# Weight remainders written over the raw unit: five raw slots and four high slots, loads released by TensorE

## What is computed

```
def first_block(x, ...):
    for layer in range(2):
        hn = rms_norm(h, norm_g[layer])
        if layer % 2 == 0:  y = pool_mixer(hn, ...)    # (m * silu(gate)) @ w_out, m from a windowed mean and w_grp
        else:               y = hgrn2_mixer(hn, ...)   # gated linear recurrence over chunks, 16 heads of 128
        h = h + y
    return rms_norm(h, final_g)

def second_block(x, c, ctx, c_ctx, ...):
    mod_l = split(silu(c) @ ada_w + ada_b, 6);  mod_c = split(silu(c_ctx) @ ada_w + ada_b, 6)
    h  = _rmsnorm(x, norm1_g) * (1 + mod_l[1]) + mod_l[0]
    hc = _rmsnorm(ctx, norm1_g) * (1 + mod_c[1]) + mod_c[0]
    z = h @ w_in;  kvc = hc @ w_in[:, 512:1536]
    att = _neighbourhood_attention(q, k, v, kc, vc, na_rpb, rows)
    sg = gelu(u) * (w_s @ _layernorm(gelu(v)) + b_s);  cv = silu(group_layernorm(dwconv31(a * sigmoid(gate))))
    x = x + mod_l[2] * (concat(att, sg, cv) @ w_out)
    x = x + mod_l[5] * _conv_ffn(_rmsnorm(x, norm2_g) * (1 + mod_l[4]) + mod_l[3], w_up, ..., w_down)
    return _rmsnorm(x, final_norm_g)
```

## Time and profile before

| | |
|---|---|
| three runs | 977.08, 981.16, 982.08 us; median 981.16 |
| the profiled execution | 976.3 us |
| its span, first to last instruction | 975.1 us |
| mean granted TensorE clock | 0.953 of 2.4 GHz |
| TensorE busy | 894.3 us (92%) |
| VectorE busy | 647.0 us (66%) |
| ScalarE busy | 412.9 us (42%) |
| rounding of units, L346, 115 times | 219.4 us busy, 1909 ns each |
| subtraction, L353, 115 times | 264.6 us busy, 2315 ns each |
| DMA | 156.49 MB, 160 GB/s over the span |

### The profile page before, as it was taken

The page is one execution under the profiler, slowest core; times in us unless marked ns, Lnnn a source line. Parts: engine busy times, 40 slices in busy tenths (PEclk is TensorE's granted clock), DMA queues, the critical chain, the costliest instruction groups (busy, mean ns, idle before and its releaser), DMA issues.

```text
span 975.1 us, 14483 instructions
## 1 busy us (share of the span) xinstructions
PE 894.3 (92%) x5949; PEld 781.7 (80%) x5949; DVE 647.0 (66%) x1011; ACT 412.9 (42%) x565; POOL 62.8 (6%) x85
## 2 busy tenths in 40 slices
PE   5999999999999999999898889886679599999995
PEld 4977878669999999999757689773337499999994
DVE  7645435457888888888876472999652766656564
ACT  6444334344343434343534243344453454444442
POOL 9200000020000000000000000700000000000000
PEclk9999999999999999999969899987789699999998
DMA  8997787972544445352505327420007255555511
GB/s 293 359 315 293 256 309 295 296 223 59 159 127 134 127 135 148 112 165 95 173 21 198 116 87 179 145 84 1 0 0 259 87 173 173 181 202 179 177 40 43
DMA packets 126282, 156.49 MB, mean 160 GB/s; under 512 B 11540, under 2 KB 100984, under 8 KB 123144
## 3 DMA queue, kind: packets, MB, share of 16 engines
q1 hardware_dynamic: 126216, 155.56, 48.7%
HBM read 154.44 MB, written 1.11 MB: 160 GB/s over the span
## 4 chain that ended last, share of the span: by engine, by line
PE 79%; DVE 13%; ACT 3%; DMA 2%; issue 2%; SPq 1%; DVEq 0%; ACTq 0%
PE acc L379 13%; PE acc L380 13%; PE acc L381 13%; PE acc L402 6%; PE acc L403 6%; PE acc L404 6%; PE misc L937 5%; DVE w_lo L353 3%; PE misc L722 2%; PE misc L1765 2%; PE misc L1764 2%; PE misc L1766 2%; DVE CA L1429 2%; PE acc L1518 2%; PE misc L1114 1%
## 5 line engine op out<-in xcount | busy, mean ns | idle before, releaser
L353 DVE TENSOR_TENSOR w_lo<-raw,w_hi 128x2048 fp32r<-128x2048 f32 x115 | 264.6, 2315 | 157.4 <-ACT w_hi L346 157.3
L379 PE MATMUL acc<-XH,w_hi 128*128 128x256 f32 x976 | 279.9, 287 | 3.4 <-ACT KT L1385 2.8
L380 PE MATMUL acc<-XL,w_hi 128*128 128x256 f32 x976 | 277.8, 285 | 0.0
L381 PE MATMUL acc<-XH,w_lo 128*128 128x256 f32 x976 | 277.8, 285 | 0.0
L346 ACT ACTIVATE w_hi<-raw 128x2048 fp32r<-128x2048 f32 x115 | 219.4, 1909 | 117.2 <-PE acc L404 51.9
L379 PEld LDWEIGHTS acc<-XH,w_hi 128*128 128x128 f32 x976 | 189.1, 194 | 7.2 <-issue 3.8
L380 PEld LDWEIGHTS acc<-XL,w_hi 128*128 128x128 f32 x976 | 189.1, 194 | 0.4
L381 PEld LDWEIGHTS acc<-XH,w_lo 128*128 128x128 f32 x976 | 188.9, 194 | 0.0
L402 PE MATMUL acc<-w_hi,XH 128*128 128x256 f32 (+1 forms) x224 | 74.1, 331 | 0.0
L974 DVE TENSOR_TENSOR KQ<-QK,DD 128x256 f32<-128x256 f32 x128 | 57.8, 452 | 23.6 <-PE misc L940 19.8
L404 PE MATMUL acc<-w_hi,XL 128*128 128x256 f32 (+1 forms) x224 | 72.5, 324 | 0.0
(11 more groups left out here) (264 smaller groups left out, 1331.6 us busy)
## 6 DMA issues: line engine op xcount, KB each, us to landing
ada_raw<-in_ada_w_dram SPq DMA_DIRECT2D x24, 1024.0 KB, 6.5
raw<-in_ffn_w_up_dram SPq DMA_DIRECT2D x22, 1024.0 KB, 5.2
raw<-in_pool_w_in_dram SPq DMA_DIRECT2D x16, 1024.0 KB, 7.1
raw<-in_hgrn_w_in_dram SPq DMA_DIRECT2D x32, 512.0 KB, 5.4
raw<-in_hgrn_w_in_dram SPq DMA_DIRECT2D x16, 1024.0 KB, 7.0
raw<-in_ffn_w_down_dram SPq DMA_DIRECT2D x11, 1024.0 KB, 4.9
raw<-in_w_in_dram SPq DMA_DIRECT2D x10, 1024.0 KB, 5.6
raw<-in_pool_w_out_dram SPq DMA_DIRECT2D x8, 1024.0 KB, 5.2
```

Source lines behind the costliest of these rows:

```text
L353: self.lo_done.up(dve.tensor_tensor(self.w_lo[j][:, 0:w], self.raw[j][:, 0:w], self.w_hi[j][:, 0:w].bitcast(F32), ALU.subtract), v)
L379: pe.matmul(o, wh[:, k, c:c + P], xh[:, k, :], start=k == 0, stop=False)
L380: pe.matmul(o, wh[:, k, c:c + P], xl[:, k, :], start=False, stop=False)
L381: m = pe.matmul(o, wl[:, k, c:c + P], xh[:, k, :], start=False, stop=k == K - 1)
```

## The change

`w_lo` loses its own memory: the subtraction of unit v writes over `raw` of the same unit. There are five `raw` slots (with `w_lo` at the same addresses) and four of `w_hi`. A raw slot is therefore in use until TensorE is done with the unit, and `load(v)` waits for that of unit v-5 (`wait_over`) in place of the subtraction of unit v-4. The ada loads move three units forward in SP's stream, from `v - 10` to `v - 7`, and the load of `g_row` in `sp_out` with them. The streams of TensorE, ScalarE, VectorE and GpSimd keep their order.

```
-        self.raw = [new(f"raw{j}", [UNIT]) for j in range(RING)]
+        raw_at = self.top
+        self.raw = [new(f"raw{j}", [UNIT]) for j in range(RAWS)]
+        self.w_lo = [self.at(raw_at + j * UNIT * 4, f"w_lo{j}", [UNIT], F32R) for j in range(RAWS)]
         self.w_hi = [new(f"w_hi{j}", [UNIT], F32R) for j in range(RING)]
-        self.w_lo = [new(f"w_lo{j}", [UNIT], F32R) for j in range(RING)]
...
     def load(self, v):
-        sp, s, j = self.nc.sync, self.unit[v], v % RING
-        if v >= RING:
-            sp.wait_ge(self.lo_done.h, self.lo_done[v - RING])
+        sp, s, j = self.nc.sync, self.unit[v], v % RAWS
+        if v >= RAWS:
+            self.wait_over(sp, v - RAWS)
...
     def hi(self, v):
-        act, j, w = self.nc.scalar, v % RING, self.unit[v].width
+        act, j, w = self.nc.scalar, v % RAWS, self.unit[v].width
         act.wait_ge(self.raw_in[j].h, self.raw_in[j][v])
         if v >= RING:
             self.wait_over(act, v - RING)
-        self.hi_done.up(act.activation(self.w_hi[j][:, 0:w], self.raw[j][:, 0:w], ACT.Copy), v)
+        self.hi_done.up(act.activation(self.w_hi[v % RING][:, 0:w], self.raw[j][:, 0:w], ACT.Copy), v)
...
     def lo(self, v):
-        dve, j, w = self.nc.vector, v % RING, self.unit[v].width
+        dve, j, w = self.nc.vector, v % RAWS, self.unit[v].width
         dve.wait_ge(self.hi_done.h, self.hi_done[v])
         self.lo_done.up(dve.tensor_tensor(self.w_lo[j][:, 0:w], self.raw[j][:, 0:w],
-                                          self.w_hi[j][:, 0:w].bitcast(F32), ALU.subtract), v)
+                                          self.w_hi[v % RING][:, 0:w].bitcast(F32), ALU.subtract), v)
...
     def sp_stream(self, v0, v1):
         for v in range(v0, v1):
-            if 0 <= v - 10 < 3 * KD:
-                self.ada_load(v - 10)
+            if 0 <= v - 7 < 3 * KD:
+                self.ada_load(v - 7)
             self.load(v)
...
-        self.sp_stream(4, 10)
+        self.sp_stream(4, 7)
         self.sp_out()
-        self.sp_stream(10, 68)
+        self.sp_stream(7, 68)
```

More of the change, by code:

```diff
@@ L20 @@
 RING = 4
+RAWS = 5
 EPS = 1e-6
@@ L226, in signal @@
             return Signal(nc, self.stack, name, self.table)
-        self.raw_in = [signal(f"raw_in{j}") for j in range(RING)]
+        self.raw_in = [signal(f"raw_in{j}") for j in range(RAWS)]
         self.hi_done = signal("hi_done")
@@ L362, in weights @@
     def weights(self, v):
-        s, j = self.unit[v], v % RING
-        return [w[j][:, 0:s.width].rearrange("p (k n) -> p k n", k=s.k) for w in (self.w_hi, self.w_lo)]
+        s = self.unit[v]
+        return [w[:, 0:s.width].rearrange("p (k n) -> p k n", k=s.k)
+                for w in (self.w_hi[v % RING], self.w_lo[v % RAWS])]
     def project(self, u, n, col, X, K, ready=None):
```

## The result

The changed kernel takes **1021.18 us** (median of 4 runs, 1020.54 to 1022.54), the kernel before 979.26 us (4 runs, 977.08 to 982.08). The ratio is 1.042, with a 95% interval of 1.040 to 1.045: 4% slower, near the 1017 of the forecast and inside its range. The profiled execution took 1022.5 us (span 1021.3, mean clock 0.926); that of before 976.3.

A forecast was written before the change was run, and what follows sets the result against it. TensorE was taken as the bound, 79% of the chain of waits. Terms +3.1, +21.1, +8.4, -0.5, +7.4 and -2.0 summed to +37.5 us on 979.2, forecast 1017 us, range 1002 to 1029.

The forecast's parts named there:

- D, on the other side: SyncE's queue: a wait does not hold the DMAs behind it, parts 4 to 6 are 0, 980 us; chance 0.04.
- Part 1: Memory: the subtraction writing over its own input costs 0, bounds -0.1 to +0.1 us.
- Part 2: Steady stages, FFN and HGRN: weight loads still arrive in time, cost 0.
- rival C: HGRN: weight units land late, 2 us in each of 16 heads, 1049 us; chance 0.05.
- Part 3: Pool stages: raw lands late behind the ada load at unit 30, delaying the norm ahead of HGRN, +3.1 us.
- rival B: TensorE's clock: restarts at the lower level after three longer stops, 3.4 us lost each, +10, 1027 us; chance 0.10.
- Part 4: Context: c_gain, c_tok, f_row and ws_in wait on SyncE behind load 67, +21.1 us.
- Part 5: x_gain waits behind load 71, delaying the residual addition: +8.4 us, with -0.5 back from the transposes.
- Part 6: Second layer, norm of VG: +1.6 us for late load 76 and 5.8 for operations held by selects, +7.4.
- Part 7: Gain before the FFN: raw 82 is loaded during attention, so its rounding comes earlier, -2.0 us.
- Rival A: Secondary terms hidden: x_gain or the selects don't hurt, 1010 us; chance 0.17.

The follow-up runs named there:

- e1: The kernel before, with only the new load wait and the changed kernel's SyncE order added, rings of four kept and nothing written in place: 1021.4 us.
- e3: Changed kernel with the context's parameters, x_gain and the bias loads issued ahead of the weight loads they stood behind: 977.2 us, ratio 0.998.
- e4: Changed kernel with seven of GpSimd's eight selects on BIAS left out, so the bias isn't masked: 1012.4 us, ratio 1.034.
- e2: Changed kernel with c_gain, c_tok, f_row and ws_in issued ahead of weight loads 65 to 67: 1003.7 us, ratio 1.025.
- e9: The kernel before, unchanged, run again for a second profile: one execution of 983.4 us.
- e6: Changed kernel with load 82 issued ahead of h_gain and last_row: 1019.0 us, ratio 1.040.
- e10: e7 with twelve unread identity products added in TensorE's stop ahead of the HGRN gate: 967.0 us, ratio 0.988.
- e11: e10 with 20, 8, 20 and 16 such unread products added in four more TensorE stops: 963.0 us, ratio 0.985.
- e8: The kernel before with rpb, SR, BS and the BIAS pieces issued ahead of load 75, nothing else changed: 971.3 us, ratio 0.991.
- e7: Changed kernel with the edits of e3 and e6, plus raw loads ahead of ada loads in the pool stages: 970.4 us, ratio 0.991.

## Why the prediction was right, and where it wasn't

- **What the change does** (D, on the other side): right. SyncE's wait holds the DMAs behind it; c_gain went at 535.9, not at 508.
- **Part 1, memory, 0**: right, by e1.
- **Part 2, steady stages, 0**: right. HGRN's 31 units and FFN's 31 are within 0.1 us in all; rival C is out.
- **Part 3, pool, +3.1**: the mechanism was right, the size was not all. TensorE starts HGRN 3.1 later than its shift so far (221.83 - 1.1 - 217.64), but the step is 5.0. The first product of HGRN in the chains of after and of before, then a window of after that starts ahead of that product, and one of before:

```profile
221.83 0.55 PE acc L383
```

```profile
217.64 0.36 PE acc L379
```

```profile
219.00:225.80 6.80, 5.92 (x26) 0.51 0.00 0
```

```profile
217.60:223.60 6.00, 5.96 (x50) 1.00 0.09 19
```

  TensorE's clock is at half until 226.0, 4.2 us into HGRN, which costs 1.9. That is rival B, at a place that the prediction didn't give it, and it meets one of its own signs of being wrong (stops that cost more than their length). In e3 and e4 the clock is at full again before that first product, and the step is 3.2.
- **Part 4, context, +21.1**: 20.3, by e2 all but 0.5 of it.
- **Part 5, x_gain, +7.9**: 8.8. VectorE's residual addition is 7.8 later; the last 1.0 is clock, and not the change's: the unchanged kernel has it too in e9 (+1.2). Windows of before, of after and of e9 over unit 68's products with x (x50 counts two of its neighbours), with a stop of 2.8 us ahead of them in all three:

```profile
582.00:590.20 8.20, 7.54 (x50) 0.79 0.50 168
```

```profile
619.00:628.10 9.10, 8.49 (x50) 0.65 0.01 2
```

```profile
583.40:592.20 8.80, 8.74 (x50) 0.65 0.51 167
```

- **Part 6, +7.4**: 7.0, with the selects as the cause of most of it (e4). In the sum the 5.8 for held operations was right (5.5 measured). The 1.6 for the late load was too much: it came 0.3 later, and the subtraction was held for 0.4. In their place 0.8 of clock was missed, so the near hit of the sum is partly luck. Rival A is out. By the rule of the Trainium skill ("SBUF — State Buffer", Who interferes with whom), told in the prediction, operations with two SBUF inputs are held by a GpSimd instruction that reads SBUF; 1.92 and 1.79 us for 0.42 agree. For one input the Trainium skill there makes it depend on whether the operation can enter a fast mode that uses both ports. The two subtract-and-scale operations, with one large input and two columns of scalars, were held (1.86 and 1.60 us for 0.41), but their 0.41 alone is no less than the 0.42 of the two-input ones, so no fast mode shows and why they were held stays open. BATCH_NORM_STATS2, with one input, ran 0.41 beside a select.
- **Part 7, -2.0: this step failed.** "In after raw 82 is loaded during attention" was read from the wait of the load alone. In SyncE's stream h_gain and last_row stand ahead of it, and they wait for the last tile of attention. The prediction applied its own rule (an issue can't pass a wait) to parameters behind loads and forgot it for a load behind parameters. e6 gives the -2.6.
- **Not in the sum**: +2.7 at the gate, which is clock (e9, e10); +0.9 in attention, less than before's two profiles differ by (5.4); +1.0 at the start, where after, e2, e3, e4 and e6, the same program up to there, differ by 1.2 among themselves.

Together, in the two profiled executions: 37.5 + 1.9 (part 3) + 2.7 (gate) - 0.8 + 0.9 - 0.4 (parts 4 to 6) + 2.2 (part 7) + 1.0 + 0.9 (start, attention) = 45.9 of the 46.2. Against the two profiled executions the sum of 37.5 is 8.7 short. The medians are 41.9 apart, since the profiled execution of after is the longest of its four and that of before among the shorter ones; so the forecast is 4.2 low and not 8.7. Which of the two is its true miss, the spread of before's executions (8.7 us from the shortest to the longest) leaves open, and that it came so near is in part luck. B was priced at 10 and weighed at 0.10; at the three stops that the change makes longest (units 64, 68, 74) the steps are 0.8 below, 0.9 above and 0.4 below the forecast, and two stops that it didn't count (pool to HGRN, gate) cost 4.6.

## What to carry to other kernels

- Before a load is made to wait for a slower engine, list what stands behind it in the same queue. Weights had 8 units of slack and lost nothing in the steady stages; the three stages with small parameters behind them grew by 36 us, and putting the parameters ahead of the wait gave all of it back with the same ring (e3).
- The rule works in both directions: for every load of which an earlier start is hoped, read what it stands behind.
- A stop of TensorE costs its length and can cost half the clock for a while behind it (3.4 or 13.6 us behind the same stop at the gate). How much of that shows differs from stop to stop (3.6 us at the one stop of e10, 0.8 in all at e11's four), so such a term belongs in the range, and a few idle products in the stop tell its size.

## What the runs showed of the hardware

- Two kernels with the same stop of TensorE (e8 and e7, 3.8 us, 474 to 477.7) and the same work behind it got 3.4 and 13.6 us at half clock. The Trainium skill ("TensorE: Matmul & The Clock Gate", Part 1: The HAM clock gate) has the moment of the change of level depend on a phase that is not the kernel's, so that it varies from run to run. In attention this case agrees (79.9 or 85.3 us for the same program, before and e9); at the gate it doesn't look so: short in three of three without the new waits, long in eight of eight with them.
- The granted clock doesn't tell all. In both windows below TensorE does its first products of 512 columns. After has 16 in 6 us at a granted 1.00, e3 has 21 at 0.72:

```profile
15.00:21.00 6.00, 6.00 (x16) 1.00 0.81 253
```

```profile
15.00:21.00 6.00, 5.69 (x21) 0.72 0.80 256
```

  After's products come every 0.43 us up to 20.7 and every 0.23 behind that, e3's change at 18.4, where its recorded clock rises. Executions of the same instructions fall into either form; it makes the difference of about 1 us at the start, and why the record of after has no half clock there stays open.
- A select of GpSimd and an operation of VectorE hold each other: beside one a select took 3.55 us in place of 1.69, and an operation of 0.42 up to 1.92.
